# Joining the RWKV output norm's stage with the FoX cache stage in a hybrid decoder step

## What is computed

```python
# rwkv branch: group norm of each head's output, a bonus, and a gate
mean = jnp.mean(o, axis=-1, keepdims=True)
var = jnp.mean(jnp.square(o - mean), axis=-1, keepdims=True)
o = (o - mean) * lax.rsqrt(var + GN_EPS)
o = o * lnx_w + lnx_b
out = ((o + bonus).reshape(b, t, A_WIDTH) * g)
# FoX over the cache
s = einsum('bqhd,bkhd->bhqk', q, k) * HEAD_DIM ** -0.5 + c_q - c_k
ob = einsum('bhqk,bkhd->bqhd', softmax(s), v)
# both
merged = sigmoid(ga) * (oa @ proj_a) + sigmoid(gb) * (ob @ proj_b)
h = h + merged @ w_out
```

## Time and profile before

| | us |
|---|---|
| median of 3 runs | 898.04 (895.63 to 901.33) |
| the profiled execution's own time | 901.33 |
| its span (first to last instruction) | 899.5 |
| PE busy | 773.7 (86%) |
| DVE busy | 374.6 (42%) |
| ACT busy | 185.2 (21%) |
| POOL busy | 149.4 (17%) |
| mean granted TensorE clock | 0.919 |
| bytes read from HBM | 211.82 MB, 243 GB/s over the span |

### The profile page before, as it was taken

One profiled execution on the slowest core, in us unless ns is written; L12 is line 12 of the kernel. 1 busy time (PEld: TensorE's weight loads), 2 busy tenths in 40 slices (PEclk: granted clock), 3 DMA queues, 4 the chain that ended last, 5 costly groups with the idle time before them and its releaser, 6 DMA issues. The chain is left out here.

```text
span 899.5 us, 20897 instructions
## 1 busy us (share of the span) xinstructions
PE 773.7 (86%) x8753; PEld 461.1 (51%) x8753; DVE 374.6 (42%) x687; ACT 185.2 (21%) x426; POOL 149.4 (17%) x300
## 2 busy tenths in 40 slices
PE   5999899989779899968886787989869997799985
PEld 2445466656566666743554565546654444444421
DVE  2130533229842245556872776624262222422213
ACT  2012122116341111012421321223111110111112
POOL 8400030007040020022042333331000000000000
PEclk9999899988988959968899899999869998999998
DMA  8622141212320302438899999986919999999993
GB/s 311 273 93 117 47 156 47 88 55 86 121 48 16 112 9 57 99 106 327 279 395 415 422 373 423 418 329 265 372 57 386 422 425 421 424 422 425 421 424 109
DMA packets 53240, 220.27 MB, mean 245 GB/s; under 512 B 21872, under 2 KB 24219, under 8 KB 28827
## 3 DMA queue, kind: packets, MB, share of 16 engines
q1 hardware_dynamic: 45456, 184.66, 53.1%
q0 software_dynamic: 7040, 34.10, 9.7%
q10 hardware_dynamic: 650, 0.18, 0.1%
HBM read 211.82 MB, written 7.09 MB: 243 GB/s over the span
## 5 line engine op out<-in xcount | busy, mean ns | idle before, releaser
L230 PE MATMUL bank<-arena 128*128 128x320 f32 x256 | 83.9, 472 | 3.7 <-PEq L112 3.7
L208 POOL DMA_DIRECT2D arena<-in_cv x112 | 59.1, 528 | 127.5 <-PE bank L1885 95.5
L546 PE MATMUL bank<-arena 128*128 128x336 f32 x224 | 71.3, 474 | 4.2 <-DVE arena L712 4.2
L2574 DVE TENSOR_TENSOR arena<-arena,bank 128x512 f32<-128x512 f32 x40 | 27.5, 688 | 108.2 <-PE bank L2362 105.2
L1522 DVE STREAM_TRANSPOSE arena<-arena 128x2048 f32<-128x2048 f32 x28 | 63.1, 2288 | 11.4 <-DMA arena<-in_ck 10.2
L2385 PE MATMUL bank<-arena 128*32 128x512 f32 x512 | 63.3, 596 | 3.5 <-DMA arena<-in_w_exp 2.8
L511 PE MATMUL bank<-arena 128*128 128x512 f32 (+1 forms) x144 | 65.0, 610 | 1.5 <-DMA arena<-in_w_zb 1.5
L230 PEld LDWEIGHTS bank<-arena 128*128 128x128 f32 x256 | 49.1, 202 | 25.3 <-issue 9.4
L546 PEld LDWEIGHTS bank<-arena 128*128 128x128 f32 x224 | 43.9, 200 | 27.4 <-issue 10.0
L1885 PE MATMUL bank<-arena 128*16 128x128 f32 x1024 | 32.9, 289 | 21.9 <-issue 18.7
L1340 ACT ACTIVATE arena<-bank 128x384 f32<-128x384 f32 (+6 forms) x63 | 25.9, 443 | 122.6 <-PE bank L230 46.2
(11 more groups left out here) (476 smaller groups left out, 1105.7 us busy)
## 6 DMA issues: line engine op xcount, KB each, us to landing
arena<-in_w_exp SPq DMA_DIRECT2D x99, 1024.0 KB, 19.9
arena<-in_ck SPq DMA_DIRECT2D x120, 256.0 KB, 6.1
arena<-in_cv POOLq DMA_DIRECT2D x112, 256.0 KB, 7.1
arena<-in_w_gate SPq DMA_DIRECT2D x8, 1024.0 KB, 4.8
arena<-in_w_za SPq DMA_DIRECT2D x7, 1024.0 KB, 6.9
arena<-in_w_zb SPq DMA_DIRECT2D x6, 1024.0 KB, 16.0
arena<-in_cv SPq DMA_DIRECT2D x16, 256.0 KB, 3.6
arena<-in_w_proj SPq DMA_DIRECT2D x8, 512.0 KB, 11.4
```

Source lines behind the costliest of these rows:

```text
L208: eng.dma_start(tile[n:P:4, :], src[bass.ds(page, 1)].rearrange("a (p j) n -> (a p) (j n)", j=4))\
L230: mm = nc.tensor.matmul(bank[b][:, 0:TM], w[:, k, a, :], xnT[:, k, NMETA:T], start=(k == 0), stop=(k == KT - 1))
L546: mm = nc.tensor.matmul(bank[j % 2][:, 0:T], w[:, k, (j % 2) * P:(j % 2 + 1) * P], xnT[:, k, :], start=(k == 0), stop=(k == KT - 1))
```

## The change

The block `rwkv_post` and its barrier are gone; its work is put at the head of the cache stage:

- PE: the heads' sums, three of the four query turns (each now has its own copy on ACT behind the squares), the sums of squares, the fourth query turn, then `scores(0)`. In `scores(0)` the spreading of the reciprocal stands between groups t = 1 and t = 2. The two gate tiles come behind `scores(0)`, in place of two fills, which move to `fills(1)` (5 tiles instead of 3). `turn_probs(0)` waits until the gate tiles are copied out.
- DVE: the transposes of the first half of sequence 1's keys stand between the norm's steps, the last two additions of the norm behind the second half of those keys (`gate_ready`).
- ACT: the gate tiles are copied behind the exponentials of b = 0, and `gates_on(1)` moves behind the copies of b = 0.
- SP: the keys of sequence 1, A0, A1, B0, keys of 2, then a wait for the store of the gate tiles, A's gates, `x_prompt`, keys of 3, B1, keys of 4.
- POOL: the bias constants, keys of sequence 1, the bonus' bias (now into `bias_o`), the gate tiles' stores, and the last 4 value pages of sequence 0.
- `oo`, `osq` and `bias_o` lie elsewhere.

```diff
-        oo = low(NPAIR, T)
-        osq = low(NPAIR, T)
+        oo = arena[:, mT_at:mT_at + NPAIR * T].rearrange("p (g t) -> p g t", g=NPAIR)
+        osq = arena[:, w_at + 2 * SLOT:w_at + 2 * SLOT + NPAIR * T].rearrange("p (g t) -> p g t", g=NPAIR)
+        assert w_at + 2 * SLOT + NPAIR * T <= soutp.offset
...
+        bias_o = pre(NPAIR, T)
...
-        with nc.Block("rwkv_post") as block:
-            @block.sync
-            def _(sp):
-                for m in range(2):
-                    load_pages(sp, key_slot(1, m), page_numbers(sp, m, 1), A["ck"])
-                for n in range(NPOST):
-                    j = GT_PAIRS + n
-                    pages = page_numbers(sp, j // 2, 0) if j % 2 else None
-                    sp.wait_ge(S("p_gt_sb"), n + 1)
-                    sp.dma_start(gates_dram[j % 2, :, j // 2, :], stage_p[j % 2]).then_inc(S(f"p_gt_out{j % 2}"), 16)
-                    if j % 2:
-                        load_pages(sp, j // 2, pages)
-                for i in range(2):
-                    sp.wait_ge(S(f"p_gt_out{i}"), 16 * (NPOST // 2))
...
         kinds += [("o", n) for n in range(4 * 2 * (NT - 1))]
-        fill_no = [0, 2, 5, 8, 11, 14, 18, 24, 28, len(kinds)]
+        fill_no = [0, 0, 5, 8, 11, 14, 18, 24, 28, len(kinds)]
...
+                for m in range(2):
+                    load_pages(sp, key_slot(1, m), page_numbers(sp, m, 1), A["ck"])
                 proj_load(sp, 0, 0)
+                proj_load(sp, 0, 1)
+                sp.wait_ge(S("kept_rw"), 16 * NPAIR * (DB + 1))
+                sp.wait_ge(S("ov_ps"), 1)
+                proj_load(sp, 1, 0)
+                key_loads(2)
+                sp.wait_ge(S("p_gt_out"), 16 * NPOST)
                 gates_load(0)
-                proj_load(sp, 0, 1)
-                key_loads(2)
+                sp.wait_ge(S("gate_ready"), 1)
+                for i in range(NT - 1):
+                    sp.dma_start(tile_of(h2, i), A["xp"][i * P:(i + 1) * P, :]).then_inc(S("xr_in"), 16)
                 key_loads(3)
-                sp.wait_ge(S("kept_rw"), 16 * NPAIR * (DB + 1))
-                proj_load(sp, 1, 0)
                 sp.wait_ge(S("fill_ps"), 4)
                 proj_load(sp, 1, 1)
-                for i in range(NT - 1):
-                    sp.dma_start(tile_of(h2, i), A["xp"][i * P:(i + 1) * P, :]).then_inc(S("xr_in"), 16)
                 key_loads(4)
...
                 ch = Chain(pool, S("cache_pool"))
+                ch(nc.gpsimd.memset(rsuf[:, DB * NPAGES * NH:], 0.0))
+                ch(nc.gpsimd.memset(hsel, 0.0))
+                ch(nc.gpsimd.tensor_tensor(hs8, ident[:, 0:NH], ident[:, 32:32 + NH], add))
+                for i in (2, 3):
+                    ch(nc.gpsimd.tensor_tensor(hs8, hs8, ident[:, 32 * i:32 * i + NH], add))
+                ch(nc.gpsimd.tensor_copy(hsel[:, :, 0:2 * DS].rearrange("p g (e q) -> p g e q", e=2),
+                                         bc(hs8.rearrange("p (g e) -> p g e", e=2), 3, DS)))
+                pool.sem_inc(S("hsel_ready"), 1)
+                for m in range(2, 4):
+                    pages = page_numbers(pool, m, 1)
+                    for n in range(4):
+                        page_load(nc.gpsimd, place[key_slot(1, m)], n, A["ck"], pages[n], S(f"kept_key{m}"))
+                for g in range(NPAIR):
+                    ch(nc.gpsimd.tensor_scalar(bias_o[:, g, :], bonus[:, g, :], prm[:, LNB + g:LNB + g + 1], None, add))
+                pool.sem_inc(S("bonus_b"), 1)
+                pool.wait_ge(S("oc_ready"), NPAIR)
                 nc.gpsimd.dma_start(vnew[0], A_vs[0]).then_inc(S("vnew_in0"), 16)
+                for n in range(NPOST):
+                    j = GT_PAIRS + n
+                    pool.wait_ge(S("p_gt_sb"), n + 1)
+                    nc.gpsimd.dma_start(gates_dram[j % 2, :, j // 2, :], stage_p[j % 2]).then_inc(S("p_gt_out"), 16)
+                pages = page_numbers(pool, 3, 0)
+                for n in range(4):
+                    page_load(nc.gpsimd, slot[7], n, A["cv"], pages[n], vpool[3])
...
                     if b:
                         pe.wait_ge(S("exp_done"), 5 * b)
+                    else:
+                        pe.wait_ge(S("hsel_ready"), 1)
+                        pe.wait_ge(S("oc_ready"), NPAIR)
                     pe.wait_ge(S("rsT_done"), b + 1)
                     for g in range(NPAIR):
...
                     for t in range(4):
+                        if b == 0:
+                            pe.wait_ge(S("qs_sb"), t + 1)
+                        if b == 0 and t == 2:
+                            pe.wait_ge(S("ov_rc"), 1)
+                            pe.wait_ge(S("qs_sb"), 4)
+                            for g in range(NPAIR):
+                                nc.tensor.matmul(bank[4 + g][:, 0:T], half_bc[strip(g), :], ovs[strip(g), :],
+                                                 start=True, stop=True).then_inc(S("ob_ps"), 1)
...
-                    pe.wait_ge(S("fill_sb"), fill_no[b + 1])
+                    if b:
+                        pe.wait_ge(S("fill_sb"), fill_no[b + 1])
+                    else:
+                        pe.wait_ge(S("p_gt_sb"), NPOST)
...
@@ -1877,6 +1812,8 @@
                     pe.wait_ge(S("pT_sb"), 4 * b + 4)
                     if b:
                         pe.wait_ge(S("ob_out"), b)
+                    else:
+                        pe.wait_ge(S("o_zero"), 2)
...
+                        if f == 0:
+                            pe.wait_ge(S("gate_ready"), 1)
...
+                for g in range(NPAIR):
+                    nc.tensor.matmul(bank[g][:, 0:T], headones, oT(g), start=True, stop=True)\
+                        .then_inc(S("om_ps"), 1)
+                def turn_queries(s, at):
+                    for i in range(4):
+                        mm = nc.tensor.matmul(bank[at][32 * i:32 * i + 32, :], ident[:, 32 * s:32 * s + 32],
+                                              q_all.rearrange("p b g c -> p (b g c)"), start=True, stop=True)
+                    mm.then_inc(S("qs_ps"), 1)
+                for s in range(3):
+                    turn_queries(s, 4 + s)
+                for g in range(NPAIR):
+                    pe.wait_ge(S("osq_ready"), g + 1)
+                    mm = nc.tensor.matmul(bank[7][strip(g), 0:T], head_cols, osq[:, g, :], start=True, stop=True)
+                mm.then_inc(S("ov_ps"), 1)
+                pe.wait_ge(S("qs_sb"), 1)
+                turn_queries(3, 4)
                 scores(0)
-                fills(0)
+                pe.wait_ge(S("o_zero"), 2)
+                for j in range(GT_PAIRS, NGT):
+                    gate_mm(pe, j, 5 + j % 2, range(KT)).then_inc(S("p_gt"), 1)
...
-                gates_on(1)
+                def keep_queries(s, at):
+                    act.wait_ge(S("qs_ps"), s + 1)
+                    nc.scalar.activation(qs.rearrange("p b (g s) c -> p b g s c", s=4)[:, :, :, s, :],
+                                         bank[at][:, :].rearrange("p (b g c) -> p b g c", b=DB, g=NPAIR), ACT.Copy)\
+                        .then_inc(S("qs_sb"), 1)
+                nc.scalar.activation(small[:, 224:225], ones[:, 0:1], ACT.Sqrt)
+                for g in range(NPAIR):
+                    act.wait_ge(S("oc_ready"), g + 1)
+                    nc.scalar.activation(osq[:, g, :], oo[:, g, :], ACT.Square).then_inc(S("osq_ready"), 1)
+                for s in range(3):
+                    keep_queries(s, 4 + s)
+                act.wait_ge(S("ov_ready"), 1)
+                nc.scalar.activation(ovs, ovs, ACT.Sqrt).then_inc(S("ort_ready"), 1)
+                keep_queries(3, 4)
+                nc.scalar.activation(small[:, 224:225], ones[:, 0:1], ACT.Exp)
+                act.wait_ge(S("bonus_b"), 1)
...
+                    if b == 0:
+                        for j in range(GT_PAIRS, NGT):
+                            act.wait_ge(S("p_gt"), j - GT_PAIRS + 1)
+                            nc.scalar.activation(stage_p[j % 2], bank[5 + j % 2][:, 0:TM], ACT.Copy)\
+                                .then_inc(S("p_gt_sb"), 1)
...
-                    if b == 2:
-                        gates_on(2)
+                    if b in (0, 2):
+                        gates_on(1 + b // 2)
...
+                dve.wait_ge(S("kept_rw"), 16 * NPAIR * DB)
+                for g in range(NPAIR):
+                    dve.wait_ge(S("om_ps"), g + 1)
+                    STT(out=oo[:, g, :], in0=bank[g][:, 0:T], scalar=-1.0 / HD, in1=oT(g), op0=mult, op1=add)\
+                        .then_inc(S("oc_ready"), 1)
                 dve.wait_ge(rsuf_in, 64)
+                dve.wait_ge(S("hsel_ready"), 1)
                 turn_bias(0)
-                ch(nc.vector.memset(bank[4][:, 0:DS], 0.0))
+                dve.wait_ge(S("ov_ps"), 1)
+                TS(ovs, bank[7][:, 0:T], 1.0 / HD, GN_EPS, mult, add).then_inc(S("ov_ready"), 1)
+                turn_keys(1, 0)
+                dve.wait_ge(S("ort_ready"), 1)
```

(20 more changed lines are left out.)

87 lines of the change are left out of this document (1 added, 86 removed).

## The result

| | before | after |
|---|---|---|
| median, 20 runs each, side by side | 901.12 | 894.01 |
| lowest and highest | 895.63, 908.24 | 888.05, 900.14 |
| ratio after / before, 95% interval | | 0.9927 (0.9905 to 0.9949) |
| the profiled execution's own time (span) | 901.33 (899.5) | 898.62 (896.8) |
| mean granted clock | 0.919 | 0.918 |

The change gains 0.7%, or 6.6 us of 901 by the ratio (the medians lie 7.1 apart). The forecast was 12 us (886.0; on the side of faster by over 1%). The sign was right, but little more than half of the size came, and what came out is within what I called no change.

The account below looks back on a forecast made before the run. Transfers were taken to bound from 455.6, with PE from 499, then the experts' ring; the front's gain is spent by scores(2), scores(4) comes 12 us earlier: 901.33 - 12 = 889.3, median 886.0, range 879 to 897.

Parts of the forecast that it names:

- what I called no change: A result within 9 us, about a per cent, of the kernel before; chance 0.27.
- What bounds, and where it can win: Transfers bound from 455.6, with PE from 499; the experts' stage only shifts, so gains come only ahead of about 560 us.
- The front: Norm's start to scores(2): scores(1) 9.5 us earlier, that gain spent by scores(2), at 454.2 to 457.7 for 455.56.
- The step of A's gates: Loaded only after the gate tiles' store, landing at 439.1; exponentials queue behind, so PE's third fill waits 6.2 us.
- the table load: ACT's table switch costs 1.28 us with no drain showing; by the skill's page the chain would be 1.4 us longer.
- The wait of 11.4 us goes: PE's wait ahead of weigh(2) vanishes, since keys of 4 are issued at 460 to 464 for 467.88.
- The missed term: From weigh(2), at 485 to 489, to scores(4): 4.1 us, two fills 3.7, a third; no wait for values.
- the 9.7 MB: B1, keys of 4, values of 2 and B's gates, taking 23.5 us, so the gates land at 484 to 488.
- It fits, with little to spare: Transfers to the values of b = 5, 49 MB, are through by about 550; the shifted kernel wants them by 553.
- Rival 1: Gain eaten where transfers bound: keys of 4 and B's gates late again, 1 to 8 us remain; chance 0.20.
- Rival 2: More is won: scores(2) at 454, no waits for values or keys behind 500, 17 us gained, 881; chance 0.08.
- Rival 3: Slower: tile 15's store and A's gates' load queue behind key pages, gates land at 455, 6 us lost; chance 0.09.

Follow-up runs that it names:

- e1: The changed kernel run again, with nothing altered; 0.9928 of before.
- e10: Changed kernel with DVE's norm multiplications ahead of the second key transpose, POOL's page numbers read earlier, and both gates_on behind exponentials of b = 1 and 3; 0.9829 of before.
- e4: Changed kernel with DVE's norm multiplications ahead of the second key transpose, and POOL reading page numbers before its waits for the gate tiles; 0.9895 of before.
- e7: Changed kernel with half of every value page of sequences 1 to 7 left out; 0.9871 of before.
- e12: Kernel before, unmerged, with B0 and x_prompt ahead of keys of 2 on SP, and gates_on behind exponentials of b = 0 and 3 on ACT; 0.9909 of before.
- e9: Changed kernel with gates_on(1) and gates_on(2) on ACT moved behind the exponentials of b = 1 and b = 3; 0.9889 of before.

## Why the prediction was right or wrong

**What bounds, and where it can win: right.** The experts' stage takes 235.3 to 238.6 us from its start to the end in every kernel above with a profile (before: 899.5 - 394.97 - 268.1 = 236.4; after 238.6; e1 235.9; e10 235.8). So what is gained ahead of it comes through, as said from the earlier trace rows, give or take these 3 us, which the same kernel shows as well (after and e1).

**The front: the end right, two steps wrong.** Up to the reciprocal all was as worked out: PE waited 0.96 us (forecast 1.2), the keys' transpose began at 405.83 - 397.15 = 8.7 from the start (forecast 9.0). The second keys came 1.2 us later than I had them, the gate tiles 1.4, and PE's idle there was 4.6 us, not 3 (3.6 in e1). That idle I had, but not the price behind it: the tiles took 10.76 us, since the granted clock was 0.57 from 418.5 to 423. So scores(1) is 6.6 us earlier and not 9.5. Then `weigh(0)`: I gave its wait for values at most 1 us; it was 2.74 (1.25 in e1), since POOL issued them 35.8 us from the start (forecast 32 to 34) and they landed 10.2 us later (forecast 7.1), with the fills after it slowed by 13.04 - 11.2 = 1.8. The step of A's gates was right in place and time (landed 45.3 from the start, forecast 44.1; load 8.2 for 8.7), but it decided nothing: the sigmoid ended at 444.79 and the fills began at 445.55. e4 shows both as rows: with the values' wait gone, the gates' wait appears (1.94). Two errors thus met in one number: that 61.4 lies in 59.2 to 62.7 is luck.

**Of the table load** I had written that no drain shows. In after ACT's next instruction again comes right behind it (444.81 + 1.28, then 446.10): the 1380 ns that the Trainium skill gives (ScalarE: Activation LUTs, What ACT_TABLE_LOAD costs) are not seen here either.

**"The wait of 11.4 us goes": right, but I took all of it.** 1.97 of it is left, and `weigh(1)` to `weigh(4)` all have about that much (1.96 to 1.97); in the program it waits there for DVE to keep the output of b - 1. What could be won there was 9.4 us.

**The missed term: this is the step that failed.** From the start of `weigh(2)` (94.5 from the start, forecast 90 to 94) to scores(4) I had 10 to 11 us (the terms are 4.1, 3.7 and a third tile, 9.7 in sum), with a wait for values put at nothing; it took 13.2. The difference is the 2.09 us for values and 6.72 us of fills, where those of b = 4 at full clock take 5.45: 3.4 us in all. e7, with half the bytes of values, has no wait there and needs 9.6 us for the same stretch (489.37 to 498.99). So against before, the change wins 9.4 us ahead of `weigh(2)` and loses 1.8 behind it (13.2 for 11.4), which is the 7.5 us at scores(4). I had counted bytes against 415 GB/s up to the gates' landing, and asked only when keys and gates come. No step of mine asked when the values of 2 land. Their issue hangs on `weigh(1)`, which the change leaves where it was, and on POOL, which needs 3.6 us for four pages. In after the four groups for b = 2 were (timeline of after, POOL):

```profile
470.68 2.25 POOL L208 DMA_DIRECT2D arena<-in_cv  x4 [17.44 <-PE bank L1822]
474.27 2.24 POOL L208 DMA_DIRECT2D arena<-in_cv  x4 [1.35 <-issue]
477.87 2.24 POOL L208 DMA_DIRECT2D arena<-in_cv  x4 [1.36 <-issue]
481.48 2.24 POOL L208 DMA_DIRECT2D arena<-in_cv  x4 [1.37 <-issue]
```

The last was issued 84.3 from the start and, in full DMA engines, had landed 99.4 from it. In before it was issued at 83.6 (478.57), only 0.7 us earlier, but its reader came 9.4 us later (`weigh(2)` at 103.9 for 94.5). The rate was mis-sized too: 386 GB/s from 460 to 502, since from 464 to 476 the engines got only 312. At that point all that was allowed had moved: keys of 4 had waited for scores(2) until 464.16, values of 2 for `weigh(1)` until 470.68. 12 us x (415 - 312) GB/s are 1.2 MB, 3 us. In this kernel a head start of transfers cannot be saved beyond the slots, and the front's early 413 GB/s was spent so. B's gates landed at 492.68, 95.5 from the start; I had 89 to 93. That sum was also a megabyte short: the 9.7 MB are the 32 pages of 256 KB and the gates' 1280 KB, without B1's two loads of 512 KB, and with them it is 10.7 MB, 25.9 us, 91 to 95. No wait hung on it: PE waited for the values first. B's gates were issued at 84.8, forecast 80 to 85, and took 10.7 us.

**"It fits, with little to spare": wrong.** `weigh(4)` waited 3.54 us for values, and 5.29 us of fills behind it instead of 3.7. Yet before paid there too (a wait of 1.58 us); from scores(4) to the experts both need about the same (152.8 before, 153.4 after).

**The rivals.** Rival 1 is what happened in size: 7.5 us of lead at scores(4), 7 at the experts, 6.6 by the ratio. Its mechanism is half right: the gates and keys were in time, the values not. In e12 the same ceiling shows with full engines. Rival 2 needed scores(2) at 454 and no waits for values; e10 has the first, still waits 5.3 us for values, and gains 15 us by its ratio (its median lies 17 below): about rival 2's size, in another kernel and not by its mechanism. Rival 3 did not occur: the store and the load met nothing (4.2 and 8.2 us). Rival 4's waits came, 4.6 us ahead of the gate tiles with DVE's 3.0 us for keys in front of them, at under half the size that it needed.

**Where the merge's gain went.** Its front is 6.6 us ahead at scores(1), even 9.5 at the start of `weigh(0)` (437.60 for 444.95), and nothing ahead at scores(2). Two fills (4.5 us) had only been moved behind scores(1); nearly all the rest went into the wait (2.7) and the slower fills (1.8) above. What it is worth when these are gone is e10 beside e12: 253.9 for 265.1 at the experts, 0.9829 for 0.9909, intervals that just do not overlap. They were run beside different runs of before, and e10's gates stand behind other exponentials than e12's, so this is an estimate of the merge's worth and not a test of it alone.

**What stays open.** What POOL's 1.36 us between two groups are worth, which set when the last values go out: no run shortened them. Why e10 gains more than e4 and e9 apart: at scores(4) it is 1.3 us ahead of e4, at the experts 4.7, and both come from single executions; the intervals of e4 and e10 touch. What holds PE 1.8 us inside the new values' matmuls in e4 and e10: the profile names nothing. And the clock's part was not isolated: no run removed the lower clock and kept the waits.

## What to carry to other kernels

Before two stages are merged to bring a transfer forward, ask what holds the transfer's issue and what stands in the way on each queue: here moving three loads on SP and two sigmoids on ACT gave as much as the merge. When a stall is priced, subtract what its neighbours keep (1.97 of 11.40), and follow every stream that shares the bytes up to its next reader, not only the one that was late: of the 11.4 us only 7.5 arrived at scores(4), since behind the 1.97 that stayed stood a wait for values of 2.09 us with slow matmuls behind it, where none had been looked for. Bytes moved early helped here only as far as there were slots to hold them.

## What the runs showed of the hardware

The granted clock fell to its lower level (about 1.2 GHz) behind short waits too, though not behind each. In after it was 0.53 from 443.1 to 450.0, behind waits of 0.16 and 2.74 us in `weigh(0)`. In e10 PE stood idle there for 0.44 and 1.86 us, and was busy 4.60 us of the 6.90 before the fall; the stretches of its PE (us; busy (x); PEclk, DMA share, GB/s):

```profile
429.50:436.40 6.90, 4.60 (x136) 0.95 1.01 410
436.40:440.00 3.60, 3.60 (x10) 0.50 1.04 424
```

So an idle of 2 to 4 us in all cost 1.3 to 2.8 us more behind it, in fills of 6.72 us for 5.45 and of 14.04 for 11.2. In e4 it did not: PE was busy 4.16 us of the 6.00 from 435 to 441, and the clock stayed at 1.00 from there through the fills. I had counted this price only behind an idle time of 6.2 us.

The rate of the DMA engines dipped in after behind scores(2). It was 350 GB/s from 464 to 467 and 286 from 467 to 470.7, while SP's key pages were the only loads being issued; then 298 to 474 and 324 to 476, with the first of POOL's value pages beside them, and 395 and more from 476 on. SP took 0.90 us for each key page of 256 KB, which is 291 GB/s, about the rate of the emptiest stretch. That the issue sets the rate there is thus likely but not shown: no run changed it, and e12 moved 412 GB/s from 462 to 474 with key pages being issued from 461.9, 0.95 us each, and values from 468.7.
